# Four gated FFNs: gate and up projections as seven block products, down projections in another order

## What is computed

```python
D_FF_2 = 2816

def swiglu(h, w_gate, w_up, w_down):
    return (jax.nn.silu(h @ w_gate) * (h @ w_up)) @ w_down

for layer in range(DEPTH):                       # DEPTH = 2
    x = x + 0.5 * swiglu(rmsnorm(x, norm_ffn1[layer]), ffn1_gate[layer], ffn1_up[layer], ffn1_down[layer])
    x = x + hybrid_mixer(rmsnorm(x, norm_mix[layer]), ...)
    x = x + 0.5 * swiglu(rmsnorm(x, norm_ffn2[layer]), ffn2_gate[layer], ffn2_up[layer], ffn2_down[layer])
return rmsnorm(x, norm_final)
```

## Time and profile before

| | us |
|---|---|
| median of 3 runs | 3692.16 (3683.97 to 3692.68) |
| the profiled execution: its time / span of its instructions | 3689.52 / 3687.7 |
| PE busy | 3602.9 (98% of the span) |
| DVE busy | 2154.0 (58%) |
| ACT busy | 1551.4 (42%) |
| one gated FFN, first matmul to last | about 350 |

### The profile page before, as it was taken

The page is one execution under the profiler, slowest core; times in us unless marked ns, Lnnn a source line. Parts: engine busy times, 40 slices in busy tenths (PEclk is TensorE's granted clock), DMA queues, the critical chain, the costliest instruction groups (busy, mean ns, idle before and its releaser), DMA issues.

```text
span 3687.7 us, 46095 instructions
## 1 busy us (share of the span) xinstructions
PE 3602.9 (98%) x17872; PEld 2938.5 (80%) x17872; DVE 2154.0 (58%) x2862; ACT 1551.4 (42%) x2222; POOL 217.6 (6%) x233
## 2 busy tenths in 40 slices
PE   9999899999999999999999999999999999999999
PEld 7777688787678887888877798888888877888887
DVE  4455666666855677435667564356335676564356
ACT  3335344436533444333455443334323464543234
POOL 0001000000200000000000310000000000310000
PEclk9999999999999999999999999999999999999999
DMA  4101256422005663425321014253435321014352
GB/s 183 35 30 40 91 160 190 136 98 92 24 35 183 169 185 115 137 103 171 109 93 49 12 64 137 103 171 109 159 104 162 95 105 49 12 57 156 103 166 91
DMA packets 57384, 394.99 MB, mean 107 GB/s; under 512 B 6480, under 2 KB 6864, under 8 KB 11984
## 3 DMA queue, kind: packets, MB, share of 16 engines
q1 hardware_dynamic: 45072, 303.97, 22.8%
q0 software_dynamic: 12096, 88.09, 10.5%
HBM read 375.26 MB, written 2.10 MB: 102 GB/s over the span
## 4 chain that ended last, share of the span: by engine, by line
PE 83%; DVE 11%; ACT 4%; issue 1%; DMA 0%; DVEq 0%; POOL 0%; SPq 0%; ACTq 0%; POOLq 0%
PE ps L534 81%; DVE split L2247 3%; ACT arena L1282 2%; PE ps L543 2%; DVE X L2251 2%; DVE arena L2251 2%; DVE arena L2247 2%; ACT split L1282 1%; DVE arena L3167 1%; ACT L1282 0%; DVE small L2263 0%; DMA ring<-in_wts 0%; DVE arena L2243 0%; DVE arena L2275 0%; DVE arena L2255 0%
## 5 line engine op out<-in xcount | busy, mean ns | idle before, releaser
L534 PE MATMUL ps<-split 128*128 128x512 f32 (+2 forms) x13260 | 3012.0, 386 | 28.8 <-DVE X L2251 12.3
L534 PEld LDWEIGHTS ps<-split 128*128 128x128 f32 x13260 | 2415.5, 188 | 544.8 <-issue 48.1
L2247 DVE TENSOR_TENSOR split<-ring,split 128x1024 fp32r<-128x1024 f32 x554 | 675.9, 1220 | 859.0 <-ACT split L1282 827.9
L1282 ACT ACTIVATE split<-ring 128x1024 fp32r<-128x1024 f32 x554 | 582.7, 1052 | 1100.8 <-PE ps L534 1053.9
L534 PE MATMUL ps<-arena 128*128 128x128 f32 (+9 forms) x3344 | 486.3, 298 | 23.4 <-ACT arena L1282 8.8
L534 PEld LDWEIGHTS ps<-arena 128*128 128x128 f32 (+2 forms) x3344 | 395.7, 191 | 98.7 <-issue 66.0
L1282 ACT ACTIVATE arena<-ps 128x512 f32<-128x512 f32 (+6 forms) x580 | 297.6, 513 | 341.3 <-PE ps L534 226.7
L2247 DVE TENSOR_TENSOR split<-arena,split 128x1024 fp32r<-128x1024 f32 (+2 forms) x210 | 250.9, 1195 | 92.1 <-ACT split L1282 74.9
L1282 ACT ACTIVATE split<-arena 128x1024 fp32r<-128x1024 f32 (+2 forms) x210 | 217.8, 1037 | 182.1 <-PE ps L534 139.3
L2251 DVE SCALAR_TENSOR_TENSOR X<-ps,X 128x512 f32<-128x512 f32 x252 | 174.3, 692 | 53.7 <-PE ps L534 29.4
L2247 DVE TENSOR_TENSOR arena<-arena 128x512 f32<-128x512 f32 (+6 forms) x246 | 174.3, 708 | 20.0 <-ACT arena L1282 8.5
(11 more groups left out here) (105 smaller groups left out, 1053.7 us busy)
## 6 DMA issues: line engine op xcount, KB each, us to landing
ring<-in_wts SPq DMA_DIRECT2D x268, 1024.0 KB, 4.8
arena<-in_wts POOLq DMA_DIRECT2D x56, 1024.0 KB, 7.9
arena<-arena POOLq DMA_DIRECT2D x14, 1024.0 KB, 10.1
ring<-in_wts POOLq DMA_DIRECT2D x14, 1024.0 KB, 7.9
ring<-in_wts SPq DMA_DIRECT2D x25, 512.0 KB, 3.5
X<-in_x SPq DMA_DIRECT2D x4, 512.0 KB, 5.7
out<-arena SPq DMA_DIRECT2D x4, 512.0 KB, 2.6
ring<-in_wts SPq DMA_DIRECT2D x2, 784.0 KB, 5.7
```

The lines of the kernel that those rows point to most:

```text
L534: return e.matmul(out, l, r, start=start, stop=stop, skip_group_check=True)
L1282: o.sig(a.activation(out, i, f, **kw), sig)
L2247: o.sig(v.tensor_tensor(out, a, b, op), sig)
```

## The change

Only the four FFNs are rewritten, with the semaphores, buffers and weight layout that this needs.

* **Gate and up** are six *blocks*: five of 512 up and 512 gate columns (w = 512), one of 256 and 256 (w = 256). A block takes all 1024 input features and all 512 tokens and is done as seven products by quarters: features in two halves of four k-tiles, tokens in two halves of 256, b = up and gate columns. Each product is 4 k-tiles x 4 (or 2) column tiles x 3 matmuls of 256 tokens.
* **Input.** The seven combinations of the input's quarters are split once per FFN and kept: four in H, three in the old weight buffers (`F.shapes`, `whole`). New weight buffers 3 to 5 serve the pieces.
* **Order of products** everywhere in the FFN: P1, P2, N5, P6, N3, P7, N4 (`ORDER`). The last two go bank by bank: all of the first bank's matmuls, then all of the second's; the five before go piece by piece.
* **U** is held in one tile instead of two. A gated block's P1 and P2 are summed in `F.part`; N5, P6, N3 are gathered in U's tile by ACT and DVE, Silu runs on ACT in place, DVE multiplies.
* **Weight sums**: t1 = b11 + b12 is made by DVE in the ring (`added_up`); t3 = b12 + b22 by a DMA and an adding DMA; t2 = b11 + t3 and t4 = b21 + t2 by adding DMAs in the ring. All eight blocks of an FFN have them (before, two units had).
* **Down**: the two units become blocks of the same kind; their forms and shapes are no longer made during the gate and up layers, except the first two forms. The order in one FFN: gate/up, gate/up, down, gate/up, gate/up, down, gate/up, gate/up (w = 256), `fd..20`, `fd..21`.

The core of the diff:

```diff
+ORDER = (("P1", "b11", "a11"), ("P2", "b21", "a12"), ("N5", "t1", "f5"), ("P6", "t2", "f6"),
+         ("N3", "b22", "f3"), ("P7", "t3", "f7"), ("N4", "t4", "a22"))
+ONTO = {"P6": "P1", "N3": "N5", "P7": "P6", "N4": "P7"}
...
+            else:
+                pc.buf = 3 + len(new) % 3
+                pc.after = new[-3] + 1 if len(new) >= 3 else None
+                new.append(n)
...
+    def block(U, forms, ready, after=None):
...
+        for r, (what, _, f) in enumerate(ORDER):
+            begun, ps = ONTO.get(what), U.of[r]
...
+            each = [(t, p) for p in ps for t in range(nt)] if r < 5 else [(t, p) for t in range(nt) for p in ps]
+            for t, p in each:
+                if t == 0:
+                    e.wait_ge(S["lo"], p.i + 1)
+                if p is ps[0] and begun:
+                    e.wait_ge(*K.read[U.name, begun, t])
...
+                if t == nt - 1:
+                    i.then_inc(S["used"], 1)
...
 # vector_program
+        def added_up(U):
...
+            for p in U.of[2]:
+                c = slice(p.q * U.w, (p.q + p.c) * U.w)
+                tt(r["b12"][:, c], r["b12"][:, c], r["b11"][:, c], ALU.add, "f_t1")
...
+        def closed(U):
+            nt = U.w // 256
+            for t in range(nt):
+                v.wait_ge(S["silu_u"], 2 * U.done + t + 1)
+                tt(at(U, t, 0), at(U, t, 0), part(t), ALU.mult, "u")
+            took(U, "P7", lambda t: at(U, t, 1), ALU.subtract, False)
...
+        extra, below, late = whole(), iter(pieces[us[0].begin + 2:]), none
+        added_up(us[0])
+        for x, U in enumerate(us):
...
+            for r in range(7):
+                if r == 0:
+                    if own:
+                        form(own["a12"])
+                    for _ in late:
+                        pass
+                    if own:
+                        shaped(own["f5"], "a21", "a22", ALU.subtract)
+                else:
+                    next(reads, None)
+                    next(reads, None)
+                if U.gated and r == 2:
+                    two(U)
+                if U.gated and r == 5:
+                    opened(U)
+                if U.gated and r == 6:
+                    closed(U)
+                for y, _ in enumerate(U.of[r]):
+                    split(next(below))
+                    if x or r or y:
+                        next(extra, None)
+                if D and r == 1:
+                    form(D.forms[0])
+                if own and r < 5:
+                    form(own[("f5", "f6", "f3", "f7", "a22")[r]])
+                    if r < 3:
+                        shaped(...)
...
+                if r == 6 and U is not us[-1]:
+                    added_up(us[x + 1])
+            late = last(U) if U.gated else reads
...
 # pool_program, a block that is not the first of its FFN
+            g.wait_ge(S["lo"], U.before.split["t3"])
+            g.dma_start(t3, b22).then_inc(S["f_base"], 16)
+            g.wait_ge(S["f_base"], U.count)
+            g.dma_start(t3, b12, accum_op=ALU.add).then_inc(S["f_t3"], 16)
+            g.wait_ge(S["lo"], U.split["b11"])
+            g.wait_ge(S["f_t1"], U.of[2][-1].sum[1])
+            g.wait_ge(S["f_t3"], U.count)
+            g.dma_start(at["b11"], t3, accum_op=ALU.add).then_inc(S["f_t2"], 16)
```

More of the change, by code:

```diff
@@ L114, in __init__ @@
         self.i, self.key, self.k0, self.nk, self.c0, self.ncol = i, key, k0, nk, c0, ncol
-        self.slot, self.landed, self.end = i % NS, 16 * (i // NS + 1), None
+        self.slot = self.landed = self.before = self.end = self.added = None
 class Form:
@@ new lines, in block @@
+        def block(name, key, p, h, kbase, c1, c2, w, at=None):
+            nonlocal blocks, summed_up
+            blocks += 1
+            B = lins[name] = Block(name, h, p, w, at, 16 * blocks)
+            B.begin, B.before = n, us[-1] if us else None
+            B.first = not us
+            us.append(B)
+            for q, k0, c0 in (("b11", 0, c1), ("b12", 0, c2), ("b21", h, c1), ("b22", h, c2)):
+                B.loads[q] = load(f"{name}/{q}", key, kbase + k0, h, c0, w)
+            slots[:] = [B.loads[q].slot for q in ("b12", "b22", "b11", "b21")]
+            per, end = 1024 // w, {}
+            for what, b, f in ORDER:
+                ld = B.loads.get({"t1": "b12", "t2": "b11", "t4": "b21"}.get(b, b))
+                of = [piece(ld, q, min(per, h - q), (f"f_{b}", B.count) if b[0] == "t" else None) for q in range(0, h, per)]
+                B.of.append(of)
+                B.pieces += of
+                end[b] = n
+            B.split = end
+            for pc in B.of[2]:
+                summed_up += 1
+                pc.sum = ("f_t1", summed_up)
+            for q, b, added in (("b11", "t2", "f_t4"), ("b12", "t1", None), ("b22", "b22", None), ("b21", "t4", None)):
+                B.loads[q].end, B.loads[q].added = ("lo", end[b]), added and (added, B.count)
+            return B
@@ new lines, in down @@
+        def down(B, a, b):
+            nonlocal shapes
+            for x, (_, _, what) in enumerate(ORDER):
+                f = Form(len(forms), what, 0, B.h, None, forms[-4].end)
+                f.end, f.gated = B.of[x][-1].i + 1, True
+                f.uses = {"a11": ("u", b.done), "a12": ("u", b.done + 2)}.get(what)
+                forms.append(f)
+                B.forms.append(f)
+            for what in ("f5", "f6", "f3", "f7"):
+                shapes += 1
+                next(f for f in B.forms if f.what == what).sum = shapes
@@ new lines, in ffn @@
+        quarters = []
+        for x, a in enumerate(("a11", "a21", "a12", "a22")):
+            fo = Form(len(forms), a, 0, 3, None, forms[-4].end)
+            fo.gated = True
+            fo.uses = (("u", us[-1].done), (us[-2].name, "N4", 1), ("u", done), (us[-1].name, "N4", 0))[x]
+            forms.append(fo)
+            quarters.append(fo)
+        row = (f"ghx{l}", f"gm_{l}", 0, 1, 0, 1024) if n_ == 1 else ("nfin", "nfin", 0, 1, 0, 1024) if l else ("gfx11", "g1_1", 0, 1, 0, 1024)
+        for c in range(2):
+            L = lins[f"fd{n_}{l}2{c}"] = Lin(f"fd{n_}{l}2{c}", 6, 512, False)
+            for kc, m in ((0, 4), (4, 2)):
+                ld = load(f"{L.name}/{kc}", f"fd{n_}_{l}", 16 + kc, m, c * 512, 512)
+                for q in range(0, m, 2):
+                    if not c:
+                        pc = Piece(n, ld, q, kc + q, 2)
+                        pc.buf = len(turned) % 3
+                        pc.after = last[pc.buf]
+                        turned.append(n)
+                        n += 1
+                    else:
+                        pc = piece(ld, q, 2, None)
+                        pc.k = kc + q
+                    L.pieces.append(pc)
+                ld.end = ("lo", n)
+                if c and kc == 0:
+                    load(*row)
+            L.tail = 3
@@ L371, in plan @@
+        lins[f"fd{n_}{l}20"].forms = quarters
+        for f in quarters:
+            f.end = n
+        lins[f"ffn{n_}{l}"] = us
     for l in range(2):
@@ L1021, in ffn, with whole @@
     def ffn(l, w, J, nxt):
[L1023 to L1035 removed]
+        nonlocal shaped
+        us = lins[f"ffn{w}{l}"]
+        shapes, begun = K.f.shapes(us[0]), shaped
+        shaped += 5
+        def whole(f):
+            n = {"f5": 1, "f6": 2, "f3": 3, "f7": 4, "a22": 5}.get(f)
+            return [(S["h_form"], begun + n)] if n else [emptied(J.name, j, f == "a12") for j in (0, 1)]
+        taken["all"] = 0
+        for U in us:
+            if U.first:
+                block(U, lambda f: shapes[f], whole, lambda r, q: J.turned(2 + q // 2) if r == 0 else None)
+            elif U.gated:
+                block(U, lambda f: shapes[f], lambda f: ())
+            else:
+                own = {f.what: f for f in U.forms}
+                block(U, lambda f: tuple(K.m.formed(own[f])), lambda f: [(S["form"], own[f].i + 1)])
+        Q = quarters(f"fd{w}{l}20")
+        lin(f"fd{w}{l}20", Q, Q.ready, of="side")
+        lin(f"fd{w}{l}21", Q, of="lin", last=nxt.last)
     def hybrid(l, J, nxt):
```

386 lines of the change are left out of this document (273 added, 113 removed).

## The result

The changed kernel takes **3898.3 us** (median of 4 runs, 3889.1 to 3899.6) against 3692.1 us before (3684.0 to 3692.7): **ratio 1.056, interval 1.0536 to 1.0581**. It is slower by 206 us; forecast were 3885 us, 13 us less. The profiled execution took 3899.6 us; its span is 3897.8.

The account below looks back on a forecast made before the run. PE, busy 98% of the span, was taken as the bound. Per FFN 61.7 us of waits less 18.3 saved gave +174 over four FFNs; with +20 for the clock, 3689.5 became 3884, forecast as 3885 us, range 3750 to 3960.

Parts of the forecast that it names:

- PE's gain: Matmuls of the whole program: 256-column ones at 0.120 us against 512-column ones at 0.227 save 73 us.
- Wait 1: Before N4 in a wide gated block: PE idle 3.65 us until DVE has read P7's first bank, 5 per FFN.
- Wait 2: Before the next block's P2: PE waits 1.05 us for DVE's `lo`, behind a down block 1.2.
- Wait 3: Down blocks: DVE bounds them, N4 to N4 takes 49.2 us instead of 38.4, 10.8 us lost, two per FFN.
- Wait 4: Narrow block (w = 256): waits before P6, N3 and N4, 4.0 us together (2 to 8).
- Wait 5: First block of each FFN: P6 late behind t2's two adding DMAs from HBM, 13.3 us lost (8 to 18).
- The sum of the waits: All PE waits in the FFNs: 61.7 us per FFN, +247 us in the account.
- The clock: Half of 24 waits over 3.6 us outside the down blocks cause a 1.7 us fall: +20 us (0 to +41).
- PE as the bound: Rival, whole kernel: DVE's slack covers the waits, only the matmuls count, 3616 us; chance 0.06.
- Half-waits: Rival, in the FFNs: the waits are about half as long, 3755 us (3700 to 3790); chance 0.16.
- Late sums: Rival, weight sums: t2, with 1 us of cover, comes late; 4 us late gives 3955 us; chance 0.13.
- a landing much before 11 us: Sign against the prediction: t2 in a wide block, issued at 9.6 and landed at 20.8, landing much earlier.

Follow-up runs that it names:

- e1: Changed kernel with the two multiplications and the reading of P7's first bank moved ahead of N4's second `lo` on DVE, wide gated blocks only: 3800.3 us, ratio 1.030.
- e3: Changed kernel with t1 added by a DMA from POOL in every block instead of two DVE instructions: 3869.1 us, ratio 1.0484.

## Why the prediction was right

The direction, the size and the mechanism held: PE saves what it was to save, and waits for DVE at the places named. That the total came within 13 us was also luck, as two terms missed by 40 us and more in opposite directions. Term by term:

- **PE's gain**: -73.1 by the slots, -73 forecast; the spacings are 0.227 and 0.120 us. The constant of about 13 ns, read from 256-column matmuls in the joins, held for all the new ones. By the Trainium skill, page "TensorE: Matmul & The Clock Gate", section "Back-to-back issue gap", they would be 0.216 and 0.109 by its formula for two warm matmuls; the trace disagrees with it, and the measurement decides.
- **Wait 1**: 3.66 for 3.65, 20 times, released by the reading of P7 as foretold, and e1 shows its cause. Two pieces of the chain had no row and were estimates, the multiplication (0.70) and ACT's start behind PE (0.25); both came out as taken, the first as 0.70 in the chain above, the second as 0.25 (P7 would have let the buffer go at 2385.71, ACT starts at 2385.96).
- **Wait 2**: 0.96 and 1.00 for 1.05 and 1.2.
- **Wait 3**: N4 to N4 in 50.5 and 51.6 us for 49.2. The order of the waits is as worked out (3.89 before P2; 4.0 forecast). But the block before begins at half clock, so that P1's second `hi` starts at 2396.89 and not near 2395.4. I let the down blocks hide falls of the clock; a fall just before one isn't hidden, since it delays DVE's list, the bound there.
- **Wait 4**: 1.54 before P6 and 1.87 before N4, 3.4 for 4.0. The 512 KB DMA for t2 took 4.7 us for my 6, which I had scaled from 10.1; the 1 MB one for t2 took 7.0 here.
- **Wait 5**: the first block takes 52.1 us from its start to N4 for 53.9, in the second FFN. In the first and the third FFN the wait stands elsewhere: before P1's second piece there are 5.91 and 5.53 us, then 4.97 and 5.94 before P6. Its release:

```profile
2706.50 1.06 ACT L1457 ACTIVATE split<-ring 128x1024 fp32r<-128x1024 f32 x1 [6.35 <-DMA ring<-in_wts]
...
2709.07 13.54 PE L652 MATMUL ps<-split 128*128 128x256 f32 x96 [5.37 <-ACT arena L1457]
```

  ACT waits for a load from HBM there. I had counted these loads as landed in time, since the earlier trace rows shows one join alone. The sum came out near enough, but for another reason in half of the cases.
- **The sum of the waits** is +207 for +247. A down block is idle 8.5 us (3.89, 1.10, 1.27, 2.20) for 10.8; what its length of 50.5 has over 38.4 beyond that is half clock. The first block of the second FFN is idle 11.7 us (1.80, 1.79, 0.31, 7.78) for 15.7. These two make most of the 40.
- **The clock** is the term that was mis-sized: **+63 for +20**, outside even its range of 0 to +41. I let 12 falls of 1.7 us happen, half of the waits outside the down blocks, from the earlier trace rows. There I had misread a row: I took the idle time before the first fall as 1.4 us, but it runs on into the next row, and PE's timeline has it as one stretch of 2.66 us, up to 723.24. Only the second fall stands behind a stretch as short as I said (1.17 us). There are 32 falls in the four FFNs, seven to nine in each: 24 outside the down blocks where I had 12, and 8 behind the waits before a down block's P2 where I had none. They are 3.4 or 6.8 us long, and cost 2.0 us in the mean (1.5 and 2.3). In the second FFN seven of the eight waits over 3.6 us were followed by one, among them the two in down blocks, and none of those up to 2.2 us was. The Trainium skill says on the same page, in "HAM oscillation — how this bites in real kernels", that PE falls to half rate in waits between bursts. The trace agrees with it for the waits over 3.6 us (32 falls behind 34 of them in the four FFNs), and I should have given it more than a half.
- **The rivals.** PE as the bound is out: 315 us idle. Half-waits would need waits under 2 us before N4; they were at full price. Late sums: t2 landed in 7.0 us in the wide blocks, where I took 11.2. This is one of the signs that I had named for being wrong (a landing much before 11 us), and it came: that step of the working was off. It changed nothing in the sum, since it only gave t2 some 5 us of cover instead of 1, and no wide gated block behind the first waited before P6:

```profile
ring<-ring POOLq DMA_DIRECT2D x28, 1024.0 KB, 10.1
ring<-arena POOLq DMA_DIRECT2D x24, 1024.0 KB, 7.0
...
ring<-arena POOLq DMA_DIRECT2D x4, 512.0 KB, 4.7
```

  These rows are the DMA issues of the changed kernel (out<-in, count, KB, median us to landing): t4, t2, and t2 of the narrow blocks. e3 shows that the rival's mechanism is real once t1 comes later.

So the small error is the difference of two larger ones. By the two profiled executions it is 16 us: waits 40 us below the forecast, clock 43 above it, and 13 of small spacings that I had not counted.

## What to carry to other kernels

An algorithm that saves TensorE an eighth of its products is paid for with VectorE's order: before adopting it, write down for each buffer that TensorE waits for what stands ahead of it in VectorE's list, because here 153 of the 206 us were the place of a few instructions and not their amount. Price each wait of several microseconds with its fall of the clock (2 us behind nearly each wait of 3.6 us and more here). Shortening instructions helps only where they stand in the row that is waited for, and moving them to GpSimd helps only if the two engines don't slow each other. And when several terms of a forecast are uncertain, compare each with its own measured number: here a total within 13 us hid two misses of 40.
